# Issuing the first four weight pieces from ScalarE's queue instead of SyncE's, in a two-block fp32 layer kernel

## The reference

```python
h = rmsnorm(h_res, g_mix_pre[l])
proj = h @ w_in[l]
u_a, c_g, b_g, v_b, gate_logits = jnp.split(proj, splits, axis=-1)
y_a = fourier_mix(u_a) @ w_fourier[l]
...
merged = gates[:, :, 0] * y_a + gates[:, :, 1] * y_b
mix_out = merged @ w_out[l]
h_res = h_res + rmsnorm(mix_out, g_mix_post[l])
```

## Time and profile before

| | |
|---|---|
| Time, median of 3 runs | 1596.18 us (1595.79 to 1596.29) |
| Profiled execution, its own time | 1596.2 us |
| Its span, first to last instruction | 1594.4 us |
| Mean granted TensorE clock | 0.998 |
| TensorE busy with matmuls | 1574.4 us, 99% of the span |
| VectorE, ScalarE busy | 69%, 35% |
| Loads of the start | 8 input tiles of 264 KB, 4 pieces of 512 KB, vectors of 4 KB and 364 KB |

### The profile page before, as it was taken

How to read it: one execution, slowest core, us unless ns; L and a number is a source line. 1 busy time by engine, 2 the same in 40 slices (tenths; PEclk the granted TensorE clock), 3 DMA queues, 4 the chain that set the end, 5 groups by cost and what they waited for, 6 DMA issues and landing times.

```text
span 1594.4 us, 24900 instructions
## 1 busy us (share of the span) xinstructions
PE 1574.4 (99%) x9688; PEld 1425.4 (89%) x9688; DVE 1107.8 (69%) x1593; ACT 564.6 (35%) x811; POOL 31.8 (2%) x63
## 2 busy tenths in 40 slices
PE   9999999999999999999999999999999999999997
PEld 8999999999999988998888898878889888888887
DVE  6334556689888842288999998954657899898224
ACT  5123233442222222253233444467335422222221
POOL 1110000000000000000001011000000000000000
PEclk9999999999999999999999999999999999999999
DMA  4442222232233233233333232222232323323332
GB/s 174 114 135 93 92 67 92 68 102 85 92 92 92 92 105 98 88 113 93 95 104 87 80 98 85 83 80 80 92 95 65 119 92 96 102 92 95 109 110 83
DMA packets 45066, 152.62 MB, mean 96 GB/s; under 512 B 5978, under 2 KB 8054, under 8 KB 44992
## 3 DMA queue, kind: packets, MB, share of 16 engines
q1 hardware_dynamic: 42912, 147.26, 29.5%
q0 software_dynamic: 2080, 4.31, 1.2%
HBM read 149.40 MB, written 4.51 MB: 97 GB/s over the span
## 4 chain that ended last, share of the span: by engine, by line
PE 79%; DVE 17%; ACT 2%; issue 1%; DMA 0%; SPq 0%; DVEq 0%
PE ps L517 65%; PE ps L527 8%; DVE work L1754 6%; DVE wlo L1391 3%; PE ps L882 1%; PE ps L555 1%; DVE work L1517 1%; DVE work L1520 1%; ACT whi L987 1%; DVE work L1552 1%; PE ps L933 1%; DVE tmp L1456 1%; DVE stage L1508 1%; PE ps L823 1%; PE ps L766 0%
## 5 line engine op out<-in xcount | busy, mean ns | idle before, releaser
L517 PE MATMUL ps<-xh,whi 128*128 128x258 f32 (+2 forms) x1800 | 495.1, 326 | 2.2 <-ACT values L1291 1.0
L517 PE MATMUL ps<-xh,wlo 128*128 128x258 f32 (+2 forms) x1800 | 490.5, 323 | 0.0
L517 PE MATMUL ps<-xl,whi 128*128 128x258 f32 (+2 forms) x1800 | 489.7, 323 | 0.0
L1391 DVE TENSOR_TENSOR wlo<-raw,whi 128x1024 fp32r<-128x1024 f32 x272 | 331.6, 1219 | 151.9 <-ACT whi L987 151.4
L987 ACT ACTIVATE whi<-raw 128x1024 fp32r<-128x1024 f32 x272 | 287.1, 1057 | 401.0 <-DMA raw<-w_dram 379.2
L517 PEld LDWEIGHTS ps<-xh,whi 128*128 128x128 f32 x1800 | 301.4, 189 | 30.1 <-issue 4.5
L517 PEld LDWEIGHTS ps<-xh,wlo 128*128 128x128 f32 x1800 | 300.6, 189 | 27.0
L517 PEld LDWEIGHTS ps<-xl,whi 128*128 128x128 f32 x1800 | 301.4, 189 | 25.8 <-issue 0.2
L1754 DVE SCALAR_TENSOR_TENSOR work<-cin,vecs,work 128x512 f32<-128x512 f32 x240 | 180.1, 751 | 6.9
L517 PE MATMUL ps<-fh,wlo 128*128 128x512 f32 x264 | 102.7, 389 | 0.0
L517 PE MATMUL ps<-fl,whi 128*128 128x512 f32 x264 | 102.7, 389 | 0.0
(11 more groups left out here) (247 smaller groups left out, 2286.8 us busy)
## 6 DMA issues: line engine op xcount, KB each, us to landing
raw<-w_dram SPq DMA_DIRECT2D x272, 512.0 KB, 3.5
bias_copies_dram<-bias_rows_dram POOLq DMA_DIRECT2D x12, 192.0 KB, 3.7
res<-x_dram SPq DMA_DIRECT2D x8, 264.0 KB, 6.4
out_dram<-res SPq DMA_DIRECT2D x16, 128.0 KB, 1.8
dftp<-dftp_dram POOLq DMA_DIRECT2D x1, 550.7 KB, 4.4
bias<-bias_copies_dram POOLq DMA_DIRECT2D x4, 128.0 KB, 2.7
bias<-bias_copies_dram POOLq DMA_DIRECT2D x8, 64.0 KB, 2.9
vecs<-vec_dram SPq DMA_DIRECT2D x1, 364.0 KB, 8.3
```

The source lines that it names most:

```text
L517: last = pe.matmul(ps[:, bank, 0:b - a], w[:, slot, cols], xx[:, k, a:b], start=start and n == 0, stop=stop and n == 2)
L1391: dve.tensor_tensor(wlo[:, slot, :], raw[:, slot, :], whi[:, slot, :].bitcast(F32), ALU.subtract).then_inc(w_split, 1)
```

## The change

The four weight pieces of the start are no longer issued by SyncE. ScalarE issues them, as the first thing it does, ahead of its table load. SyncE issues input tile 0, then the gain vector, then tiles 1 to 7 and the rest of the vectors. Semaphores, waits and everything behind stay as they are.

```diff
         @block.sync
         def _(sp):
-            sp.dma_start(vecs[:, 0:KD], vec_in[:, 0:KD]).then_inc(gain_landed, 16)
             for k in range(KD):
                 sp.dma_start(res[:, k, :], x_in[:, k, :]).then_inc(x_landed[k], 16)
-                if k % 2 == 0:
-                    sp.dma_start(raw[:, k // 2, :], w_in[k // 2]).then_inc(w_landed[k // 2], 16)
+                if k == 0:
+                    sp.dma_start(vecs[:, 0:KD], vec_in[:, 0:KD]).then_inc(gain_landed, 16)
             sp.dma_start(vecs[:, KD:], vec_in[:, KD:]).then_inc(vec_landed, 16)
...
+            for s in range(SLOTS_W):
+                act.dma_start(raw[:, s, :], w_in[s]).then_inc(w_landed[s], 16)
             act.preload_act_table(ACT.Sqrt)
             act.wait_ge(gain_landed, 16)
             cut_input()
```

## The result

| | before | change | difference |
|---|---|---|---|
| Median | 1596.3 us (20 runs) | 1599.9 us (20 runs) | +3.6 us, 0.23% |
| Lowest to highest | 1595.79 to 1599.59 | 1598.99 to 1601.04 | |
| Profiled execution | 1596.2 us | 1599.23 us | +3.03 us |
| Its span | 1594.4 us | 1597.4 us | +3.0 us |

The ratio is 1.002, with a 95% interval from 1.0013 to 1.0027. The change makes the kernel slower, by a little more than the 0.2% that I took as the limit of what can be told from no change. In the second measurement, on another occasion, the change came to 1599.86 us and the kernel before to 1596.36.

The account below looks back on a forecast made before the run. TensorE was taken to bound the kernel, with start delays carried through one for one. The single term, +1.6 us for the late third input tile, on 1596.2 gave 1597.8 us; range 1594.9 to 1599.9.

Parts of the forecast that it names:

- the clock case: Rival, TensorE's start: a late first pass lets the granted clock fall, costing 2.1 us, 1599.9 us in all; chance 0.17.
- within 0.2%: Whole kernel: the time stays within 3.2 us of the kernel before; chance 0.83.
- my own signs of being wrong in the mechanism: Profile after: `xh` 0 before 5, TensorE's run without a gap from the second tile, or clock below 1.00 before 12 us.
- The kernel's bound, and that a shift carries through: TensorE, 79% of the chain, paces everything from 9.18; a shift at 10 us reaches the end one for one.
- ScalarE's issues are hidden: ScalarE's start: four issues take 1.9 us, covered by the 2.92 us it waited for tile 0.
- The gain vector behind tile 0: Loads at the start: its 128 small rows alternate with piece 1, 1.3 us more, landing at 6.3 against 2.65.
- Tile 2 behind the weights: Start, strict alternation with the weights: tile 2 lands at 10.3 against 8.0, third input tile at 11.9, +1.9 us.
- My +1.9 before weighting: TensorE's third input tile: strict alternation gave +1.9 us; +1.6 us was taken after weighing other byte orders.
- served by whole loads: Bound of the tile 2 term: each queue served a whole load in turn, 1.3 us earlier, given as +0.5.
- the +2.9 in the range: Upper end of the forecast's own case for the late third input tile, +0.5 to +2.9, chance 0.48.
- the +2.7: Bound of the tile 2 term: full starting cost of 1.1 us paid on top of strict alternation.
- Everything behind tile 2 is in time: After the third input tile: ScalarE needs 2.3 us per tile pair and piece, TensorE 2.9, so nothing else is late.

Follow-up runs that it names:

- the second profile of the change: The changed kernel measured once more, nothing altered: 1599.86 us (10 runs), its profiled execution 1600.82 us.
- the table-first kernel: The change with ScalarE's table load put ahead of its four issues of weight pieces: 1600.22 us, ratio 1.0024.
- the runs with the clock held: The change with more matmuls on ones in TensorE's idle time at the start: 1598.14 us, ratio 1.0011.
- The one-queue kernel: The kernel before with all loads on SyncE's queue, in about the order in which the change's loads landed: 1600.82 us, ratio 1.0028.
- the three others with a late tile 2 and no filling: No added matmuls on ones: the kernel before reordered on one queue, 1600.82 us; the change with gain vector first, 1599.48, or table load first, 1600.22.
- a cold start: The kernel before without its matmuls on ones, loads and cuts unchanged: 1597.91 us, ratio 1.001.

## Why the prediction was right and where it was off

The measured 1599.9 us lies at the very end of my range, and that it is not outside is luck: the end was drawn through the middle of the clock case, to which I gave little weight. The likeliest number, 1597.8, was 2.1 us too low, and "within 0.2%", which I gave 0.83, is not what came. Of my own signs of being wrong in the mechanism, a granted clock below 1.00 ahead of 12 us came in the second profile of the change.

- **The kernel's bound, and that a shift carries through: right.** 3.17 us at 29.48 became 3.0 at the end of the span.
- **ScalarE's issues are hidden: right.** They took 2.46 us, more than my 1.9; the table-first kernel had ScalarE free 1.4 us sooner and gained nothing.
- **The gain vector behind tile 0: mis-sized.** I had 1.3 us for it, with `xh` 0 at 6.3. Tile 0 landed 4.3 us after its issue at 0.75, at 5.05, and the vector at 5.4, so it added 0.35. Why the same rows cost 1.6 us at the head of the queue and 0.35 behind tile 0 is open. Therefore the first pass was not late at all (forecast +0.8, measured 0.0), and the second tile by 0.48 and not 0.7. It didn't count, since tile 2 decides.
- **Tile 2 behind the weights: right.** Forecast: landing at 10.3, third input tile at 11.9. Measured: 9.88 and 11.56; 11.96 in the repeated run. My +1.9 before weighting, and +1.6 after it, stand against 1.54 in the profile and 1.8 us in the runs with the clock held (1598.14 against 1596.36). The one-queue kernel shows that the order of the bytes alone does it. Tile 7 came at 13.99; forecast 13.8. That forecast used 400 GB/s throughout, which two queues did move from 5 us on; the kernel before moved only 317 to 395 from 4 to 9 us, of which my working makes nothing. Two bounds of this term were added up loosely: served by whole loads it is +0.6 (1.9 less 1.3) and not +0.5, and the +2.9 in the range has no working beyond the +2.7.
- **Everything behind tile 2 is in time: right.** No wait follows 11.56.
- **The clock: the step that failed.** I had it as a rival with 0.17 and gave it 2.1 us for its price and 1599.9 us as its time. That is what happened. The clock fell in both profiles of the change and in the three others with a late tile 2 and no filling, and 1.7 us went away when TensorE was kept busy. The price was nearly right (1.6 and 2.6 in the two profiles, 1.7 between the medians, 1.5 for a cold start, 2.2 on one queue); the chance was wrong, and so was the condition. I had tied the fall to a late first pass, and the first pass came at 7.22, on time; the waits for the second and the third input tile were enough. I argued from the kernel before, where the clock held between 5.54 and 9.18, that it would probably hold again. But by my own landings the sparse stretch would last to 11.9, six passes in six us, and the one fall in the trace had come within a us or so of TensorE's last work. The likelier case should have been the sum of both terms, 1596.2 + 1.6 + 2.1 = 1599.9.

The clock fell with TensorE busy 0.44 of the us ahead of it. The Trainium skill says in "TensorE: Matmul & The Clock Gate", Part 1, that the clock is set by how busy TensorE has been recently; the runs agree with it, and I had used it only for a rival.

Between 9 and 12 us the two queues together moved 401 to 415 GB/s, and one queue moved 421 in the us from 9. The Trainium skill says in "DMA: Bandwidth & Descriptors", section Issuing engines are not separate DMA queues, that loads from several engines interleave on the same DMA engines and that a second issuer saves only issue time. From 9 us on these rates agree. From 5 to 9 us they don't: 414 GB/s with two queues against 338 with one, for about the same order of bytes, though SyncE's issues ran well ahead of the transfers in both.

## What to carry to other kernels

A second queue added nothing to the stream once that ran at some 400 GB/s (from 9 us on), and some 60 to 80 GB/s in the us from 5 to 9. But it gives away the order, since the loads that can wait then share the stream with those that can't, and here that cost more. Before moving loads to another queue, write down which bytes would be ahead of the one with the least to spare. And a new wait on TensorE early in a run has two prices, the wait and a fall of the clock after it; the second here was as large as the first, and matmuls on ones in the gap took it away in ten of eleven runs.

## What the runs showed that I had not expected

- A table load doesn't hold up the DMA issues behind it on ScalarE: with the load at 0.74 for 1.28 us the issues began at 0.77. The other way round, four issues put the table load off to 3.23.
- The clock column can't be relied on at the start. In the kernel without matmuls on ones it says 1.00 for stretches in which the passes ran at the pace of half clock:

```profile
11.00:12.00 1.00, 1.00 (x7) 1.00 1.04 407
12.00:13.00 1.00, 1.00 (x6) 1.00 1.04 418
```

  At the start of a kernel the spacing of the matmuls is the better witness.
- The moment of the fall is not tied to the kernel's own timing. The two profiles of the change have it in the us from 12 and in the us from 10, and pieces 0 and 1 on ScalarE's queue gave a kernel that loses 1.5 to 2 us in two of eleven runs and nothing in the others. The kernel before's own high runs, some 1.3 to 3.7 us over its median, read a lower mean granted clock in all but one case; none of them was profiled, so that their clock falls in the start is likely and not shown.
